# A two-block transformer kernel on one core: convolution taps dealt anew among three engines, attention as a pipeline over heads

## What is computed

```python
u = glu(conv_in)                                   # 512 channels
u = causal_depthwise_conv(u, w, b)                 # 31 taps per channel
u = silu(layernorm(u))
conv_out = u @ w_conv_branch + b_conv_branch
# attention, 8 heads of 64, causal, stick-breaking
z = q k^T / 8
log_1m = where(mask, log_sigmoid(-z), 0)
rev_excl = reverse_cumsum(log_1m) - log_1m         # sum over later keys: the suffix sum
a = where(mask, exp(log_sigmoid(z) + rev_excl), 0)
att = a @ v
merged = sigmoid(g_conv) * conv_out + sigmoid(g_att) * (att @ w_att_branch)
```

## Time and profile before

| | us |
|---|---|
| median of 3 runs | 1040.56 |
| lowest and highest | 1038.27, 1042.57 |
| the profiled execution, its own time | 1045.19 |
| its span | 1043.5 |
| PE busy | 957.3 (92%) |
| DVE busy | 505.4 (48%) |
| ACT busy | 330.3 (32%) |
| POOL busy | 32.3 (3%) |

### The profile page before, as it was taken

The page is one execution under the profiler, slowest core; times in us unless marked ns, Lnnn a source line. Parts: engine busy times, 40 slices in busy tenths (PEclk is TensorE's granted clock), DMA queues, the critical chain, the costliest instruction groups (busy, mean ns, idle before and its releaser), DMA issues.

```text
span 1043.5 us, 14199 instructions
## 1 busy us (share of the span) xinstructions
PE 957.3 (92%) x5910; PEld 681.7 (65%) x5910; DVE 505.4 (48%) x886; ACT 330.3 (32%) x523; POOL 32.3 (3%) x39
## 2 busy tenths in 40 slices
PE   5999799999999999998989799778888989999997
PEld 5997535443434444443434788768778979999885
DVE  5684513122322222222312676986777657766742
ACT  4723211101000000100001554425557645554541
POOL 1000000000000000000000000012420000000000
PEclk9999799999999999999999899988999989999999
DMA  9947699999999999999999522442422533545401
GB/s 359 409 187 291 272 376 416 421 430 430 430 430 430 431 431 429 430 430 431 430 428 428 221 81 82 162 161 81 143 100 82 193 151 105 219 162 180 184 1 40
DMA packets 23621, 289.52 MB, mean 277 GB/s; under 512 B 2560, under 2 KB 4864, under 8 KB 6016
## 3 DMA queue, kind: packets, MB, share of 16 engines
q1 hardware_dynamic: 22832, 286.98, 67.4%
q10 hardware_dynamic: 720, 1.57, 0.4%
HBM read 287.49 MB, written 1.05 MB: 277 GB/s over the span
## 4 chain that ended last, share of the span: by engine, by line
PE 71%; DVE 14%; ACT 6%; DMA 5%; issue 4%; SPq 0%; DVEq 0%; ACTq 0%
PE ps L270 70%; DVE wl L266 5%; DMA ring<-in_moe 4%; DVE arena L1457 3%; ACT wh L259 2%; DMA ring<-in_w_in 1%; PE ps L959 1%; ACT arena L1466 0%; DVE arena L547 0%; DVE arena L1634 0%; DVE arena L352 0%; DVE arena L1641 0%; ACT arena L1665 0%; ACT arena L1669 0%; ACT arena L1667 0%
## 5 line engine op out<-in xcount | busy, mean ns | idle before, releaser
L270 PE MATMUL ps<-ring,arena 128*64 128x512 f32 x1232 | 341.5, 598 | 8.6 <-issue 8.5
L270 PEld LDWEIGHTS ps<-ring,arena 128*64 128x64 f32 x1232 | 109.5, 138 | 170.1 <-issue 167.9
L266 DVE TENSOR_TENSOR wl<-ring,wh 128x1024 fp32r<-128x1024 f32 x150 | 180.2, 1231 | 63.3 <-ACT wh L259 63.2
L270 PE MATMUL ps<-arena 128*64 128x512 f32 (+5 forms) x432 | 163.3, 533 | 13.2 <-ACT arena L1675 11.6
L259 ACT ACTIVATE wh<-ring 128x1024 fp32r<-128x1024 f32 x150 | 150.8, 1049 | 33.1 <-PE ps L270 29.7
L1070 DVE SCALAR_TENSOR_TENSOR arena<-ps,arena 128x512 f32<-128x512 f32 x16 | 12.0, 750 | 216.5 <-PE ps L270 216.5
L270 PEld LDWEIGHTS ps<-arena 128*64 128x64 f32 (+2 forms) x432 | 59.1, 149 | 61.4 <-issue 44.3
L270 PE MATMUL ps<-up_h,wh 128*128 128x256 f32 x352 | 88.3, 286 | 4.6 <-DVE up_l L1866 4.6
L270 PE MATMUL ps<-up_l,wh 128*128 128x256 f32 x352 | 87.8, 285 | 0.0
L270 PE MATMUL ps<-h_h,wh 128*128 128x256 f32 x256 | 69.2, 302 | 5.0 <-DVE wl L266 2.5
L270 PEld LDWEIGHTS ps<-up_h,wh 128*128 128x128 f32 x352 | 67.5, 192 | 4.9 <-issue 4.9
(11 more groups left out here) (260 smaller groups left out, 1531.1 us busy)
## 6 DMA issues: line engine op xcount, KB each, us to landing
ring<-in_moe SPq DMA_DIRECT2D x77, 2048.0 KB, 22.1
arena<-in_moe SPq DMA_DIRECT2D x19, 2048.0 KB, 26.6
ring<-in_w_in SPq DMA_DIRECT2D x12, 2048.0 KB, 8.8
ring<-in_w_up SPq DMA_DIRECT2D x11, 2048.0 KB, 7.7
ring<-in_w_dn SPq DMA_DIRECT2D x5, 2048.0 KB, 7.8
ring<-in_w_out SPq DMA_DIRECT2D x4, 2048.0 KB, 14.9
ring<-in_w_pg SPq DMA_DIRECT2D x2, 2048.0 KB, 21.5
ring<-in_w_in SPq DMA_DIRECT2D x2, 1024.0 KB, 10.4
```

Source lines behind the costliest of these rows:

```text
L266: e.tensor_tensor(wl(i), raw_piece(i), wh(i), SUB).then_inc(*lo.up(i))
L270: return e.matmul(o, l, r, start=first, stop=final, skip_group_check=True)
```

## The change

The taps are dealt anew: VectorE takes all 31 of chunk 0 and taps 0 to 15 of chunk 1 (47), ScalarE and GpSimd the other 77. Of these ScalarE writes the first tap of chunks 2 and 3 straight to `CA` and the other 75 as products, now into a ring of 11 places, and GpSimd adds the 75. The taps stand in the programs in small portions, and what is left of the lists stands behind attention. In attention TensorE's step becomes: values of head s-2, scores of head s, gate chunk, suffix sum of head s-1, gate chunk; the last values stand alone behind the steps. The low and high parts in a step are other pieces than before. In the merge two branch products stand ahead of the first mean and two more ahead of the second.

```diff
-        TP = A(19712, 4, 256)
+        TP = A(19712, 11, 256)
...
-        todo["dve"] = [(j, k) for k in range(31) for j in range(3)]
-        todo["act"] = [None] + list(range(1, 31))
+        todo_v = [x for k in range(16) for x in ((1, k), (0, k))] + [(0, k) for k in range(16, 31)]
+        todo_a = [x for k in range(31) for x in ((2, k), (3, k))] + [(1, k) for k in range(16, 31)]
+        todo_p = todo_a[2:]
...
+        def taps_act(e, n):
+
+            for j, k in todo_a[:n]:
+                src = CU[:, j, k:k + 256]
+                if k == 0:
+                    e.activation(CA[:, j, :], src, ACT.Identity, scale=dw(j, k), bias=vcol("dw_b", j)).then_inc(*tap_a.up(j, k))
+                else:
+                    i = todo_p.index((j, k))
+                    if i >= 11:
+                        e.wait_ge(*tap_p.at(*todo_p[i - 11]))
+                    e.activation(TP[:, i % 11, :], src, ACT.Copy, scale=dw(j, k)).then_inc(*tap_a.up(j, k))
+            del todo_a[:n]
...
         def in2_pe(e):
...
-            e.wait_ge(*r45.at(0))
-            e.wait_ge(*q_.at(2))
+            e.wait_ge(*k_.at(0))
             for i in range(2):
-                k = e.transpose(ps[2][:, i * 128:i * 128 + 128], R45[:, i * 128:i * 128 + 128], ident)
+                k = e.transpose(ps[4][:, i * 128:i * 128 + 128], R45[:, i * 128:i * 128 + 128], ident)
             k.then_inc(*rcol.up("turned"))
-            for i in range(2):
-                wide(e, ps[i][:, :], "in2", 4, i, H5H, H5L)
 
         def in2_act(e):
...
-            split_hi(e, IN2 + 16 + 8)
-            e.wait_ge(*rc.at(0))
-            for i in range(2):
-                e.wait_ge(*proj.at("in2", 4, i))
-                e.activation(VT[:, i, :], ps[i][:, :], ACT.Copy, scale=RC[:, i:i + 1]).then_inc(*vv.up(i))
-            split_hi(e, IN2 + 16 + 10)
+            split_hi(e, IN2 + 14)
+            e.wait_ge(*glu.at(3))
+            e.wait_ge(*cpad.at(0))
+            for j in range(8):
+                split_hi(e, IN2 + 15 + j)
+                taps_act(e, 3)
...
         def in2_dve(e):
...
-                taps_dve(e, 6)
+                taps_dve(e, 2)
                 split_lo(e, IN2 + 8 + j + 7)
             for j in range(4):
                 e.wait_ge(*proj.at("in2", 3, j))
                 e.tensor_tensor(KT[:, j, :], ps[4 + j][:, 0:256], R45, M).then_inc(*k_.up(j))
-                taps_dve(e, 6)
+                taps_dve(e, 2)
                 split_lo(e, IN2 + 12 + j + 7)
             e.wait_ge(*rcol.at("turned"))
-            e.tensor_copy(RC, ps[2][:, 0:256].rearrange("p (i n) -> p i n", i=2)[:, :, 0]).then_inc(*rc.up(0))
-            split_lo(e, IN2 + 16 + 10)
-            taps_dve(e, 13)
+            e.tensor_copy(RC, ps[4][:, 0:256].rearrange("p (i n) -> p i n", i=2)[:, :, 0]).then_inc(*rc.up(0))
+            split_lo(e, IN2 + 22)
 
         def att_pe(e):
...
+            wide(e, ps[0][:, :], "in2", 4, 0, H5H, H5L)
+            scores(0)
+            wide(e, ps[1][:, :], "in2", 4, 1, H5H, H5L)
+            for s in range(1, 9):
+                if s >= 2:
+                    values(s - 2)
                 if s < 8:
                     scores(s)
-                if 1 <= s < 8:
-                    gates()
-                if s >= 1:
-                    suffix(s - 1)
-                gates()
-                if s >= 1:
-                    values(s - 1)
+                gates(2 * s - 2)
+                suffix(s - 1)
+                gates(2 * s - 1)
+            values(7)
...
         def att_dve(e):
...
+            masked_scores(0)
+            taps_dve(e, 2)
+            split_lo(e, IN2 + 23)
+            softplus(0)
+            split_lo(e, IN2 + 24)
+            taps_dve(e, 7)
+            for s in range(1, 9):
                 if s < 8:
...
+                    masked_scores(s)
+                split_lo(e, IN2 + 23 + 2 * s)
+                taps_dve(e, 1)
+                if s < 8:
+                    softplus(s)
+                gates(2 * s - 2)
+                less_suffix(s - 1)
+                split_lo(e, IN2 + 24 + 2 * s)
+                taps_dve(e, 1)
+                if s % 2 and s >= 3:
+                    rest((s - 3) // 2)
+                gates(2 * s - 1)
+            rest(3)
             taps_dve(e, 1000)
 
         def att_act(e):
...
+            taps_act(e, 4)
+            v(0)
+            log_part(0)
+            split_hi(e, IN2 + 24)
+            taps_act(e, 4)
+            v(1)
+            for s in range(1, 9):
                 if s < 8:
...
+                    log_part(s)
+                split_hi(e, IN2 + 23 + 2 * s)
                 taps_act(e, 2)
...
+                if s % 2 and s >= 3:
+                    rounded_part((s - 3) // 2)
+                x = AB[:, (s - 1) % 2, :]
+                e.wait_ge(*s_c2.at(s - 1))
+                e.activation(x, x, ACT.Exp).then_inc(*s_at.up(s - 1))
+                split_hi(e, IN2 + 24 + 2 * s)
                 taps_act(e, 2)
+            rounded_part(3)
             taps_act(e, 1000)
 
         def att_pool(e):
...
+            for j, k in todo_p:
+                e.wait_ge(*tap_a.at(j, k))
+                if k > 1:
+                    e.wait_ge(*((tap_p if (j, k - 1) in todo_p else tap_v).at(j, k - 1)))
+                e.tensor_tensor(CA[:, j, :], CA[:, j, :], product(j, k), ADD).then_inc(*tap_p.up(j, k))
...
         def merge_pe(e):
...
             e.wait_ge(*sg_in.at(15))
...
             branch(0)
+            branch(1)
+            mean(e, ps[0][:, 0:256], CA, inv512, [conv_end(j) for j in range(4)], "mu")
+            branch(2)
+            branch(3)
             mean(e, ps[1][:, 0:256], TMP, inv512, [ca_sq.at(x) for x in range(4)], "var")
-            for j in range(1, 8):
+            for j in range(4, 8):
                 branch(j)
```

More of the change, by code:

```diff
@@ L1458, in taps_dve @@
                                            op1=ADD).then_inc(*tap_v.up(j, k))
[L1459 to L1467, removed]
+            del todo_v[:n]
         def in2_pe(e):
@@ L1612, in att_dve, with masked_scores, softplus, less_suffix @@
-        def att_dve(e):
[L1613 to L1617, removed]
+                gates(2 * s - 2)
+                suffix(s - 1)
+                gates(2 * s - 1)
+            values(7)
+        def att_dve(e):
+            def masked_scores(h):
+                e.wait_ge(*s_sc.at(h))
+                if h >= 2:
+                    e.wait_ge(*s_c2.at(h - 2))
+                e.scalar_tensor_tensor(out=ZM[:, h % 2, :], in0=ps[2 + h % 2][:, 0:384], scalar=0.125, in1=nm, op0=M,
+                                       op1=ADD).then_inc(*s_zm.up(h))
+            def softplus(h):
+                x = AB[:, h % 2, :]
+                e.wait_ge(*s_zm.at(h))
+                e.wait_ge(*s_ln.at(h))
+                e.scalar_tensor_tensor(out=x, in0=ZM[:, h % 2, :], scalar=0.0, in1=x, op0=MAX, op1=ADD).then_inc(*s_sp.up(h))
+            def less_suffix(h):
+                e.wait_ge(*s_suf.at(h))
+                e.tensor_tensor(AB[:, h % 2, :], ZM[:, h % 2, :], ps[4 + h % 2][:, 0:384], SUB).then_inc(*s_c2.up(h))
+            def rest(j):
+                e.wait_ge(*at_h.at(j))
+                e.tensor_tensor(ATL[:, j, :], ps[6 + j % 2][:, 0:256], ATH[:, j, :], SUB).then_inc(*at_l.up(j))
+            def gates(g):
@@ L1618, in gates @@
                 n, j = chunks[g]
                 dst, jj = (SGC if n < 2 else SGA), 4 * (n % 2) + j
+                if g == 0:
+                    e.wait_ge(*x4.at(7))
                 e.wait_ge(*proj.at("in2", 5 + n, j))
                 e.tensor_tensor(dst[:, jj, :], ps[j % 2][:, 0:256], R45, M).then_inc(*sg_in.up(g))
-                split_lo(e, n_piece[("in2", 5 + n), j] + 7)
-            for s in range(9):
-                if s < 8:
[L1626 to L1648, removed]
@@ L1649, in att_dve @@
+            rest(3)
             taps_dve(e, 1000)
         def att_act(e):
[L1652 to L1659, removed]
-                if s < 8:
[L1661 to L1675, removed]
-                taps_act(e, 2)
[L1677 to L1680, removed]
-                    e.activation(ATH[:, j, :], ps[6 + j % 2][:, 0:256], ACT.Copy).then_inc(*at_h.up(j))
@@ new lines, in log_part @@
+            def log_part(h):
+                x = AB[:, h % 2, :]
+                e.wait_ge(*s_zm.at(h))
+                if h >= 2:
+                    e.wait_ge(*s_val.at(h - 2))
+                e.activation(x, ZM[:, h % 2, :], ACT.Abs).then_inc(*s_abs.up(h))
+                e.wait_ge(*s_abs.at(h))
+                e.activation(x, x, ACT.Exp, scale=-1.0).then_inc(*s_exp.up(h))
+                e.wait_ge(*s_exp.at(h))
+                e.activation(x, x, ACT.Ln, bias=1.0).then_inc(*s_ln.up(h))
@@ L1696, in build, with conv_end @@
         AB0, CB0 = n_piece[("ab", 0), 0], n_piece[("cb", 0), 0]
+        def conv_end(j):
+            return (tap_p if j else tap_v).at(j, 30)
         ca_c = sig("ca_c", range(4))
```

39 lines of the change are left out of this document (16 added, 23 removed).

## The result

The changed kernel takes 1054.16 us (median of 4 runs, 1053.02 to 1055.31), the kernel before 1040.17 on the same chip: a ratio of 1.0133, 95% interval 1.0109 to 1.0157, slower by 14.0 us. 1053.6 was forecast.

A forecast was written before the change was run, and what follows sets the result against it. Attention was taken as bound by VectorE and ScalarE waiting for each other, not TensorE's work, with GpSimd turns slowing VectorE. Merge delays +11.4 and +1.6 made +13.0 us: 1040.56 to 1053.6, range 1036 to 1062.

The forecast's parts named there:

- Step 1: End of the projection: VectorE rounds of 3.40 us beside GpSimd's additions, head 1's masked scores at 693.2 us.
- The turns: VectorE instructions with two SBUF inputs and GpSimd additions shut each other out, 0.48 us charged per turn.
- The one open bound: Softplus in attention, never seen meeting an addition: charged +0.48 us a step, 3.4 in seven; other bound 0.
- Step 2: Attention: the VectorE and ScalarE ring of waits plus three turns makes a step 11.16 us, against 10.28.
- Step 3: Behind attention: 13 left products keep GpSimd adding until 18.1 us into step 8; convolution ends at 789.4 us.
- Step 4: Merge: slow first mean puts subtraction +11.4 us; branch products delay second mean, root 5.2 behind subtraction, +1.6.
- the ratio of a stage after a like idle time: First mean in the merge: 1.5 us of chunks times 1.85 after TensorE's idle time, 2.8 us.
- Rival (d): Merge: TensorE stays slow after idling, branch products and second mean nearly double, +4 us, 1057.6; chance 0.68 together with forecast.
- The sum: Whole kernel: +11.4 at the merge's subtraction and +1.6 at the root make +13.0 us.

The follow-up runs named there:

- the kernel with both edits: Changed kernel with ScalarE's high parts one piece earlier and 3 and 3 of its products in a step instead of 2 and 2: 1027.69 us (0.9861).
- the fastest kernel: The kernel with both edits, branch products 2 and 3 behind the second mean, VectorE's taps moved from projection end and between heads 0 and 1 into steps: 1018.66 us.

## Why the prediction was right

**Step 1 held.** A round of 3.40 was forecast, 3.44 came; head 1's masked scores were set 38.5 us behind the last gating product (693.2 less 654.72), and came at +38.9. The turns are real, and the run with short additions prices them at 10.1 against 9.7. (The prediction miscounted one thing that the sum doesn't use: the 48 taps and the 32 removed are those up to the copy of `RC` at 687.05; before the last key at 683.21 stand 42.) The one open bound, whether softplus pays, is settled: 1.09 in the trace, 1.0 from start to start, against 0.47 to 0.49 without additions. By the rule of the Trainium skill (SBUF — State Buffer, "Who interferes with whom"), VectorE work with two SBUF inputs pays and work with one does not; the trace agrees in both halves: tap, softplus and low part pay, the reads from PSUM stay at 0.41.

**Step 2 held.** 11.16 against 11.1, the idle times 2.7 and 1.6 against 2.65 and 1.54. That the high part's place and not TensorE's work makes the step was argued from the written order; the run with early high parts shows it by undoing that alone. What the forecast didn't see is how large that piece is: 17.8 us for three shifted numbers, more than the whole loss. What the pipeline over heads costs or brings by itself is not shown, since no run has it with the old deal of taps; with the early high parts in both, the changed kernel, whose list then still stands behind attention, is no faster than the one before (1036.41 and 1034.69).

**Step 3 held, two terms too small.** The convolution ended 19.15 us into the last step (785.90 less 766.75) for 18.1. Half of the difference is there before the list:

```profile
764.50 4.62 POOL L1713 TENSOR_TENSOR arena<-arena 128x256 f32<-128x256 f32 x4 [3.19 <-ACT arena L1464]
```

```profile
766.75 1.78 DVE L266 TENSOR_TENSOR wl<-ring,wh 128x1024 fp32r<-128x1024 f32 x1
```

In the last step ScalarE has no logarithm to make, its products come early, and four additions run together. The step's first low part meets them and takes 1.70 from start to start instead of 1.14, which puts the subtraction of the suffix sum at 2.91 for 2.45. The other half is the run itself, 15 additions in 13.72, 0.91 each, where 0.88 and 0.80 were taken; no row splits the run, so which of the two prices was off stays open. Without the list 8.2 us come back.

**Step 4: size right, cause half wrong.** "Two branch products now stand ahead of the second mean" was to bring the root from 3.66 to 5.2 behind the subtraction; it came 5.56 behind. The second mean was over 5.1 behind it:

```profile
792.11 1.89 PE L270 MATMUL ps<-arena,ones 128*128 128x256 f32 x8
```

But the root at 794.48 came not with it, at 794.00, but when ScalarE had made its four high parts, 3.88 us between squares and root. I had not counted that the change moves two of these there. The forecast's 5.2 holds 2.85 and 1.9 for TensorE and some 0.45 from the end of the second mean to the root, near the 0.54 of before (784.02 to 784.56); but there too ScalarE was still at its high parts; where none stand in between, the root follows the mean by 0.04 (798.06 and 798.10). So high parts and branch products hold the root almost equally long, which is why moving the high parts alone brought only 0.1 here (the second mean then ended 5.4 behind), and moving the products alone nothing in the kernel with both edits. The first mean's 2.93 against 2.8, by the ratio of a stage after a like idle time, held.

**Rival (d)** came in for a quarter of its 4 us: the two branch products ahead of the second mean took 3.8 us for 2.85, with a granted clock of 0.50 from 786 to 789, but the second mean itself 1.89.

**The sum** was +13.0. The trace has +14.8 at the convolution's first branch product: 1.3 too little at the subtraction, most of it step 3, 0.3 at the root, and 0.1 behind it. The medians have +14.0. That they come within 0.6 us of the forecast is partly luck: the profile of after is 1.2 us shorter behind that product, where the two programs are the same, and this takes back most of what the sum had missed.

**Left open.** The gating product that I count from started between 649.00 and 654.72 us in the profiles, though no kernel differs up to there; whether that goes with the kernel or with the execution, no run shows. It is one reason why counted stretches and medians of single edits differ. The early high parts bring the first branch product from +154.4 to +132.0, 22.4 us, and the medians 17.8. The two moves of taps bring it from +123.0 to +119.6, 3.5 us, and the medians 9.2; the two profiles are 11.1 apart, and the other 7.6 lie in nearly equal parts before that gating product and behind the first branch product, where the kernels are the same; the profiled execution of the fastest kernel was also the fastest of its five. So its 1018.66 is measured, but not all of the last 9 us is shown to come from the taps. Nor was a kernel tried that leaves VectorE no taps behind attention: the fastest one still has five there, behind GpSimd's last addition and ahead of the first mean (746.96, 2.56 us).

## What to carry to other kernels

When a program is reordered, count for every prepared piece how far ahead of its user it is made, and cost a step as the ring of waits that results; the engine with the most work may not be in it, as TensorE, 91% busy, was not in the changed kernel's. Charge each GpSimd addition in SBUF as one turn (here about 0.5 us) to whatever VectorE does beside it with two SBUF inputs, and the reverse: VectorE's work that is moved into GpSimd's last additions delays the end that waits for them. Work dealt to a slower pair of engines has to be used up before the stage ends, since what is left of its list stands on the path.

## What was not expected of the hardware

A turn under a standing backlog costs a 1.14 us low part as much as a 0.40 us tap: 1.68 and 0.88 from start to start, about 0.5 each. The granted clock fell to 0.65 from 689 to 708.6, the stretch with TensorE's wait of 7.6 us, and the 8 matmuls of values and scores took 3.12 right behind it, for 1.71:

```profile
696.60 3.12 PE L270 MATMUL ps<-arena 128*64 128x256 f32 x8 [7.62 <-ACT arena L1702]
```

```profile
689.00:708.60 19.60, 12.01 (x62) 10.71 (x62) 11.24 (x16) 10.51 (x19) 6.69 (x6) 0.65 0.15 65
```

In the steps of after this cost nothing, since TensorE isn't in their ring; where TensorE does set the step, one slow stretch shows as a step of 10.6 to 11.9 us. And work in front of a short critical matmul group cost less than it took: the two branch products took 4.1 us ahead of the second mean (792.07 to 796.17), and the root lay 8.40 behind the start of the first mean with them, 7.70 without (789.70 to 798.10, 788.97 to 796.67), since without them the group ran in 3.78 us for 1.89, at a granted clock of 0.50.
